# The side input's gate by seven block products in place of eight, in an fp32 two-layer encoder on one core

## The reference, cut to what matters

```python
for i in range(DEPTH):                       # DEPTH = 2, D_MODEL = 1024
    h = h + mixer(rmsnorm(h, norm_mix_g[i]))
    h = h + expert_choice_moe(rmsnorm(h, norm_ffn_g[i]), ...)
    gate = sigmoid(rmsnorm(h, norm_ple_g[i]) @ ple_w_gate[i])     # (256 x 1024) @ (1024 x 1024), twice
    h = h + (p[i] @ ple_w_proj[i]) * gate
return rmsnorm(h, final_norm_g)
```

## Time and profile before

| | |
|---|---|
| Median of 3 runs | 1766.92 us (1766.44 to 1767.38) |
| The profiled execution's own time | 1766.45 us |
| Its span, first to last instruction and transfer | 1764.7 us |
| PE busy | 1636.6 us (93%) |
| DVE, ACT, POOL busy | 572.2, 453.6, 133.0 us |
| Mean granted TensorE clock | 0.982 of 2.4 GHz |
| Read from HBM | 446.87 MB |

### The profile page before, as it was taken

One profiled execution on the slowest core, in us unless ns is written; L12 is line 12 of the kernel. 1 busy time (PEld: TensorE's weight loads), 2 busy tenths in 40 slices (PEclk: granted clock), 3 DMA queues, 4 the chain that ended last, 5 costly groups with the idle time before them and its releaser, 6 DMA issues.

```text
span 1764.7 us, 21301 instructions
## 1 busy us (share of the span) xinstructions
PE 1636.6 (93%) x9045; PEld 847.3 (48%) x9045; DVE 572.2 (32%) x1030; ACT 453.6 (26%) x990; POOL 133.0 (8%) x113
## 2 busy tenths in 40 slices
PE   7999899999889979999999899898999998899788
PEld 4464544443233324578875677854444432333233
DVE  3562311121201213388971356633111212012032
ACT  3232211101011105422125565442111010111053
POOL 2000000000000002052404231000000000000000
PEclk9999999999999999999999999999999999999999
DMA  7008379999999995012120000264799999999931
GB/s 251 1 1 333 120 316 427 427 427 428 427 425 427 428 424 191 1 48 96 50 94 1 1 3 2 97 282 171 286 428 427 427 429 428 424 427 428 426 132 48
DMA packets 50909, 450.34 MB, mean 255 GB/s; under 512 B 4931, under 2 KB 7199, under 8 KB 25599
## 3 DMA queue, kind: packets, MB, share of 16 engines
q1 hardware_dynamic: 50288, 448.67, 61.3%
q0 software_dynamic: 288, 0.22, 0.0%
q10 hardware_dynamic: 239, 0.09, 0.0%
HBM read 446.87 MB, written 2.10 MB: 254 GB/s over the span
## 4 chain that ended last, share of the span: by engine, by line
PE 68%; DMA 15%; DVE 7%; ACT 5%; issue 4%; POOL 1%; SPq 1%; DVEq 0%; ACTq 0%; POOLq 0%
PE banks L1830 28%; PE banks L1241 13%; DMA ring<-in_moe_w_up 7%; PE banks L1369 5%; DMA ring<-in_moe_w_down 5%; PE banks L1463 3%; PE banks L1721 3%; PE banks L1809 3%; PE banks L1858 2%; DVE misc L2171 2%; DMA ring<-in_moe_w_gate 2%; PE banks L1886 2%; PE banks L1324 1%; PE banks L1428 1%; PE banks L1513 1%
## 5 line engine op out<-in xcount | busy, mean ns | idle before, releaser
L1830 PE MATMUL banks<-ring,misc 128*64 128x512 f32 x2048 | 458.2, 598 | 34.0 <-DMA ring<-in_moe_w_up 21.0
L1830 PEld LDWEIGHTS banks<-ring,misc 128*64 128x64 f32 x2048 | 146.6, 138 | 318.3 <-issue 276.6
L1830 PE MATMUL banks<-ring,hid_t 128*64 128x512 f32 x976 | 217.5, 595 | 16.1 <-DMA ring<-in_moe_w_down 13.4
L1241 PE MATMUL banks<-ring,xt 128*128 128x512 f32 (+1 forms) x448 | 189.8, 585 | 1.0 <-ACT xt L830 0.5
L2537 DVE TENSOR_TENSOR work<-work,banks 128x512 f32<-128x512 f32 x32 | 33.6, 1052 | 476.7 <-PE banks L1830 476.7
L1191 ACT ACTIVATE misc<-banks 32x512 f32<-32x512 f32 x64 | 37.6, 587 | 458.3 <-PE banks L1830 457.9
L1830 PEld LDWEIGHTS banks<-ring,hid_t 128*64 128x64 f32 x976 | 68.4, 137 | 155.5 <-issue 138.1
L1241 PEld LDWEIGHTS banks<-ring,xt 128*128 128x128 f32 x448 | 84.8, 190 | 104.0 <-issue 102.9
L2552 DVE COPY misc<-banks 32x512 f32<-32x512 f32 x64 | 44.2, 691 | 226.0 <-PE banks L1830 225.6
L678 POOL TENSOR_TENSOR ring<-ring 128x1024 f32<-128x1024 f32 x24 | 59.6, 2486 | 738.9 <-DMA ring<-in_gdn_w_in 666.4
L2171 DVE SCALAR_TENSOR_TENSOR misc<-ring,conv_w,misc 128x512 f32<-128x512 f32 x96 | 92.2, 960 | 3.4
(11 more groups left out here) (327 smaller groups left out, 1677.0 us busy)
## 6 DMA issues: line engine op xcount, KB each, us to landing
ring<-in_moe_w_gate SPq DMA_DIRECT2D x64, 2048.0 KB, 22.3
ring<-in_moe_w_up SPq DMA_DIRECT2D x64, 2048.0 KB, 24.0
ring<-in_moe_w_down SPq DMA_DIRECT2D x58, 2048.0 KB, 25.0
ring<-in_gdn_w_in SPq DMA_DIRECT2D x8, 2048.0 KB, 8.4
ring<-in_ple_w_gate SPq DMA_DIRECT2D x4, 2048.0 KB, 21.4
ring<-in_moe_w_down SPq DMA_DIRECT2D x6, 1024.0 KB, 23.2
ring<-in_mla_w_out SPq DMA_DIRECT2D x2, 2048.0 KB, 23.4
misc<-in_moe_w_down SPq DMA_DIRECT2D x2, 2048.0 KB, 21.4
```

The costliest lines, as they stand in the source:

```text
L1241: mm = pe.matmul(psum[:, banks.bank(st, i), 0:cols], lhs(k), rhs(k), start=(k == 0), stop=(k == n - 1))
L1830: mm = pe.matmul(psum[64 * f:64 * f + 64, bank, :], tokens(4 * kh + k), w[k][:, k, f * HALF:(f + 1) * HALF], start=(kh == 0 and k == 0), s ...
```

## The change

```diff
+            def ple_pool(l):                              # POOL; l=0 ahead of gdn_pool(), l=1 behind it
+                b11, b12, b21, b22 = pg_w_in(l)
+                t1, t2 = pg_t(l)
+                pool.wait_ge(moe_sem["w_used"], NPIECE * (l + 1))
+                for f in range(2):
+                    wait_use(pool, f"ple_g{f}{l}")
+                pool.tensor_tensor(t1, b12, b11, ALU.subtract).then_inc(sum_weights, 1)
+                pool.wait_ge(sum_weights, 4 * l + 1)
+                pool.tensor_tensor(t2, b22, t1, ALU.subtract).then_inc(sum_weights, 1)
+                pool.tensor_tensor(b12, b22, b12, ALU.subtract).then_inc(sum_weights, 1)
+                pool.wait_ge(sum_weights, 4 * l + 3)
+                pool.wait_ge(*lay[l].s_pg.full(out_no(P2, 1) + 1))
+                pool.tensor_tensor(b21, b21, t2, ALU.subtract).then_inc(sum_weights, 1)
...
+        def norm_pair(act, name, sigmoid):                # ACT, blocks 2 and 3
...
+            for j in js:
+                sigmoid(j, 1)
+            for x, j in enumerate(js):
+                square(j, 1)
...                                                        # Identity with eps on the half's sum
+            sigmoid(NT, 0)
+            square(NT, 0)
+            sigmoid(NT + 1, 0)
+            act.activation(half_ss[:, 2 * NJ:2 * NJ + 1], eps[:, :], ACT.Sqrt)
+            root(NT, n + 5)
+            square(NT + 1, 0)
+            root(NT + 1, n + 7)
+            scaled(NT)
+            scaled(NT + 1)
...
-                for i in range(8):                        # ACT
-                    act.wait_ge(*L.s_pg.full(i + 1))
...
-                    act.activation(gate[:, i % 2, :], psum[:, banks.bank(L.s_pg, i), :],
-                                   ACT.Sigmoid).then_inc(L.s_pg.freed(i)[0], 1)
-                    if i % 2:
-                        load_sqrt()
-                        norm_act(act, ("mix1", "last")[l], i // 2)
+                for t in range(NT):
+                    copy_out(L.s_pg, out_no(P1, t), pg_p1[:, t, :])
...
+                for j, f in PLE_ORDER[0:4]:
+                    sigmoid(j, f)
+                load_sqrt()
+                for j in range(NT):
+                    norm_act(act, ("mix1", "last")[l], j)
+                norm_pair(act, ("mix1", "last")[l], sigmoid)
...
-                for key in (f"ple_g0{l}", f"ple_g1{l}"):  # PE
-                    wait_use(pe, key)
-                for i in range(8):
...
+                wait_use(pe, f"ple_g0{l}")
+                gate_product(P1, a11, b11)
+                L.s_pxt.wait_read(pe, KD - 1)
+                gate_product(P2, a12, b21)
+                pe.wait_ge(sum_tokens, 4 * l + 2)
+                pe.wait_ge(sum_weights, 4 * l + 2)
+                gate_product(P6, s2, t2)
+                gate_product(P5, s1, t1)
+                pe.wait_ge(sum_tokens, 4 * l + 4)
+                gate_product(P3, a12, b22)
+                pe.wait_ge(sum_weights, 4 * l + 4)
+                gate_product(P7, a21, b12)
+                gate_product(P4, a22, b21)
...
+                dve.tensor_tensor(s1, a21, a22, ALU.add)  # DVE; waits and counts left out here
+                dve.tensor_tensor(s2, s1, a11, ALU.subtract)
+                dve.tensor_tensor(a21, a11, a21, ALU.subtract)
+                for t in range(NT):
+                    gate_add(pg_c11[:, t, :], pg_p1[:, t, :], P2, t)
+                dve.tensor_tensor(a12, a12, s2, ALU.subtract)
+                for t in range(NT):
+                    gate_add(pg_q[:, t, :], pg_p1[:, t, :], P6, t)
+                for t in range(NT):
+                    gated_add(t, 0)
+                for t in range(NT):
+                    gate_add(pg_w[:, t, :], pg_q[:, t, :], P5, t)
+                for t in range(NT):
+                    gate_add(pg_c12[:, t, :], pg_w[:, t, :], P3, t)
+                    gated_add(t, 1)
...
+                for t in range(NT):
+                    norm(normed, t)
+                    gate_add(pg_w[:, t, :], pg_w[:, t, :], P7, t, False)
+                    gate_add(pg_q[:, t, :], pg_q[:, t, :], P7, t)
+                for t in range(NT):
+                    gated_add(NT + t, 1)
+                for t in range(NT):
+                    gate_add(pg_q[:, t, :], pg_q[:, t, :], P4, t)
+                    gated_add(NT + t, 0)
+                for t in range(NT):
+                    norm(normed, NT + t)
```

More of the change, by code:

```diff
@@ L120, in add, with skip @@
         self.order.append((stage, i))
+    def skip(self, n):
+        for _ in range(n):
+            self.order.append(self.order[-self.banks])
     def bank(self, stage, i):
@@ L414, in trunk_kernel @@
             if l == 1:
-                s_xt1 = stage("xt", KD, AV, before=prev.s_pxt)
+                s_xt1 = stage("xt", KD, AV, before=prev.s_pg)
                 s_ba = stage("gdn_ba", 1, ["dve"])
@@ L451, in trunk_kernel @@
             L.s_xt = stage("ffn_xt", KD, AV, before=s_xt1 if l else s_xt0)
-            L.s_lg = stage("router", 1, ["dve"], before=prev and prev.s_ib)
+            L.s_lg = stage("router", 1, ["dve"], before=prev.s_ib if l else s_vec)
             L.s_lgt = stage("router_t", 1, ["dve"], before=L.s_lg)
@@ L459, in trunk_kernel @@
             L.s_pxt = stage("ple_xt", KD, AV, before=L.s_xt)
-            L.s_pg = stage("ple_gate", 8, ["act"], before=prev and prev.s_pg)
+            L.s_pg = stage("ple_gate", 14, ["act"] * 2 + ["dve"] * 12, before=L.s_pxt)
+            banks.skip(2)
         vec_in, tab_in, out_done = sem("vec_in"), sem("tab_in"), sem("out_done")
@@ L773, in added, with square, root, scaled @@
             else:
-                eng.wait_ge(ple_added, 2 * NJ * int(prev[3]) + 2 * j + f + 1)
+                eng.wait_ge(ple_added, 2 * NJ * int(prev[3]) + PLE_ORDER.index((j, f)) + 1)
+        def norm_pair(act, name, sigmoid):
+            i = norm_no[name]
+            js = range(NT, NJ)
+            part = [half_ss[:, 2 * j:2 * j + 2] for j in js]
+            n = 4 * (NJ * i + NT)
+            def square(j, f):
+                added(act, name, j, f)
+                act.activation(work[:, f * HALF:(f + 1) * HALF], h[:, j, f * HALF:(f + 1) * HALF], ACT.Square, scale=1.0 / 32,
+                               accum_out=half_ss[:, 2 * j + f:2 * j + f + 1]).then_inc(sq_done, 1)
+            def root(j, count):
+                act.wait_ge(sq_done, count)
+                act.activation(rstd[:, j:j + 1], half_ss[:, 2 * j:2 * j + 1], ACT.Sqrt,
+                               bias=half_ss[:, 2 * j + 1:2 * j + 2]).then_inc(sq_done, 1)
+            def scaled(j):
+                if name != "last":
+                    act.wait_ge(rstd_done, NJ * i + j + 1)
+                    dst, src = half(j, 0, name)
+                    act.activation(dst, src, ACT.Copy, scale=rstd[:, j:j + 1]).then_inc(xn_act, 1)
+            for j in js:
+                sigmoid(j, 1)
+            for x, j in enumerate(js):
+                square(j, 1)
+                act.wait_ge(sq_done, n + 2 * x + 1)
+                act.activation(half_ss[:, 2 * j + 1:2 * j + 2], half_ss[:, 2 * j + 1:2 * j + 2], ACT.Identity,
+                               bias=eps[:, :]).then_inc(sq_done, 1)
+            sigmoid(NT, 0)
[7 more added lines that the diff above has]
+            scaled(NT + 1)
         def norm_act(act, name, j):
             i = norm_no[name]
-            for f in range(2):
+            f_last = 0 if name in ("mix1", "last") and j >= NT else 1
+            for f in (1 - f_last, f_last):
                 added(act, name, j, f)
@@ L2559, in _ @@
                 xt_out(dve, "dve", L.s_pxt, ROW_PLE + 8 * l)
[L2560 to L2573 removed]
+                a11, a12, a21, a22 = pg_tokens
```

94 lines of the change are left out of this document (69 added, 25 removed).

## The result

| | before | after |
|---|---|---|
| Median (runs, range), us | 1766.38 (8, 1764.73 to 1767.38) | 1773.41 (8, 1771.18 to 1777.40) |
| The profiled execution, us | 1766.45 | 1771.56 |
| Its span, us | 1764.7 | 1769.8 |
| Mean granted TensorE clock | 0.982 | 0.978 |

The ratio after to before is 1.0046, interval 1.0036 to 1.0056: slower by 7.0 us, more than the 0.2% that a measurement of this kernel can tell from nothing.

A forecast was written before the change was run, and what follows sets the result against it. The prediction took PE to bound the gate stage, with no slack behind it; its terms, -13.8 + 13.8 + 3.4 + 6.5 = +9.9 us, gave 1776.8 us, own range 1772 to 1782, 8 in 10 within 1768 to 1785.

The forecast's parts named there:

- Matmuls: Gate product: 56 matmuls in place of 64 in each layer, 6.9 us less a layer, -13.8 us in all.
- The start: Ahead of each gate: three POOL sums hold DVE's norm scalings, so the stage starts +7.1 us (layer 0), +6.7 (layer 1) later.
- The end of layer 1: After layer 1's last gate matmul: DVE has three times the work, last norm ends 9.0 us behind it, +3.4 us.
- DVE busy without a pause: Sign expected in the profile after: DVE has no pause over the last 12 us.
- The end of layer 0: After layer 0's gate: 22 more transposes stand behind block 2's norm, partly at a slow clock; +6.5 us, between +4 and +8.
- The mixer's sums and POOL's fourth: Beside the gate's matmuls: these POOL sums delay DVE's additions, but DVE catches up by P3's second output; nothing, up to 2 us otherwise.
- The sum: All terms: -13.8 + 13.8 + 3.4 + 6.5 = +9.9 us, giving 1776.8 us.
- scalings not held: Rival: POOL's sums hold DVE's norm scalings little or not, so the gate starts on time; -3.9, 1763.0 us; chance 0.12.
- reciprocal held: Rival: POOL's sums also hold the norms' 128x1 reciprocal ahead of the gate; +8 more, 1785 us; chance 0.1.
- ends that overlap better: Rival: start as forecast, but stage ends cost less (layer 1 +0.5, layer 0 +3); 1770.6 us; chance 0.12.
- wait for t2 or s2: Rival: POOL's weight sums come so late or long that PE waits for them in the gate; chance below 0.03.
- the end at E + 10: Layer 1's end: with a 1380 ns drain per ACT table load, the stage ends 10 us after the last gate matmul.

The follow-up runs named there:

- e1: The kernel before with the gate product over seven of its eight feature chunks, 56 matmuls a layer, nothing else: 1754.42 us, ratio 0.9941.
- e3: The changed kernel with one wait more: POOL starts its weight sums only after the last transposes ahead of the gate; 1764.21 us, ratio 0.9994.
- e8: The changed kernel with late POOL sums, block-by-block transposes, DVE additions between norms, mixer sums held until the last norm, six spare matmuls: 1766.10 us, ratio 1.0008.
- e2: Second experiment: the kernel before with only POOL's three 128x2048 weight sums added ahead of each gate, used by nobody; 1777.58 us, ratio 1.0067.
- e10: The kernel before with 223 spare waits in PE's program among layer 0's experts, nothing else; 1766.76 us, ratio 1.0001.
- e5: The kernel of e1 with eight spare fp32 matmuls at the start of PE's program; 1751.47 us, ratio 0.9914.

## Why the prediction was right, and where its sizes were off

The sign and the mechanism came as forecast: slower, since POOL's sums take at the start what the matmuls give, and the ends make the rest. The size was 7.0 us where +9.9 was forecast (1773.4 for 1776.8; the other 0.5 us is the kernel before, 1766.4 in eight runs for 1766.9 in three).

- **Matmuls**, -6.9 a layer: measured -6.94 in the kernel after, and -6.86 with nothing else changed (e1).
- **The start**, +7.1 and +6.7: measured +6.65 and +6.38. The term was too large by 0.8 in all. Three sums of 4.6, twice 0.3 us of turn-taking and 0.27 behind were to take 14.7 us; they took 14.12 (672.15 to 686.27). A sum is 4.50 where nothing holds it, and the turns cost 0.33 in all, not 0.6: from start to start there are 4.59 and 4.53 us. The 0.3 of rows 7 was that of L2171, an instruction of 0.75 us with two inputs; the scalings are 0.49 with one. t2 was ready 19 us before P6, not 10, as the forecast's own times give too (684.4 and 703.9). The Trainium skill, "SBUF — State Buffer", "SBUF: two separate sides", has DVE and POOL share ports under an exclusive lock, which a DVE instruction with two inputs takes only if both lie in SBUF. The trace agrees: the two additions with a PSUM input at 676.86 took 1.27 together inside POOL's sum L713.
- **The end of layer 1**, +3.4: measured +2.6. The order of events was the forecast's, step for step: norm(0)'s reciprocal at E - 8.7 for E - 8.8, the first addition of P4 ending at E - 0.2 for E + 0.5, norm(3)'s end at E + 8.2 for E + 9.0. The mis-sized term is the length of an instruction in a row of several. Two additions are 1.28 in a row of their own, but the next instruction starts 1.19 behind their start (1751.24, 1752.43). I added lengths where starts follow each other more closely; from norm(0)'s reciprocal to the end of P4's first addition it took 8.5 us instead of 9.3. "DVE busy without a pause" was not so: it has pauses of 1.03, 0.71 and 0.35 us behind E, all for ACT.
- **The end of layer 0**, +6.5: measured +6.2. Block 2's scaling was to end at E + 7.5, and 30 transposes start at E + 7.4. The granted clock in that window was 0.74 on average, between the levels of 1.2 and 2.4 GHz, and the transposes took 0.172 us each against 0.12 at the full clock. From the first of them to C it was 4.43 us, where before it was 0.51: 3.9 for the 22 that had come in between, 2.6 + 1.5 in the forecast.
- **The mixer's sums and POOL's fourth**, put at nothing: these were not free. The sums L734 begin at S + 18.5 and end at S + 30.1, as forecast, and hold DVE's first four gated instructions at 0.99 to 2.83. "By my count of its queue it has caught up" held in the kernel after: that addition starts at S + 34.6 in both layers, though only layer 0 has the mixer's sums; with the sums a little later against the stage (e3) it cost 2.8. The term was right by a margin that I had not worked out.
- **The sum.** Terms measured: -13.9 + 13.0 + 2.6 + 6.2 = +7.9. The medians say +7.0, and between the sum of the stages and the median the other kernels differ by up to 2.3 (e1), apart from e8, which slowed the mixer. So 2.0 of the 2.9 us are in the terms, and the last 0.9 is in what varies between executions.

The rivals: scalings not held (1763.0), out by the second experiment; reciprocal held, out by its 0.16 in every trace; ends that overlap better (1770.6), a tenth of its way in layer 0, over a quarter in layer 1. With 1773.4 the time lies about halfway between the forecast and this rival; that it came so near is in part what varies between executions. PE did not wait for t2 or s2.

ACT's table load in the end of layer 1 went from 1762.11 to 1763.40, and the next activation began with its end. No drain stands in the rows beside it, and the end at E + 10 did not come, which the prediction worked out from the figures of the Trainium skill, "ScalarE: Activation LUTs", "What ACT_TABLE_LOAD costs" (1283 ns and a drain of 1380).

**Open.** Why the stretch between the stages varies from 940.8 to 947.1 us (e8 left out) in kernels whose engines do the same work there, and why PE pauses 1.8 to 3.2 us in some of them. The kernels before, e2 and e10, with eight products, have none; all the others do, except e5.

## What to carry to other kernels

Work put on an idle engine is not free if it holds the instructions of an engine on the critical chain: here a POOL sum of 4.5 us turns each DVE scaling of 0.49 us that it meets into one of 2.7 to 4.6 us, and a norm's chain meets one per block. Before adding such sums, list which DVE instructions without an operand in PSUM fall into their time (the reciprocal of 128x1 was free), and give that work to ACT or start the sums behind them; then look where the sums that were behind have gone, since in e3 and e8 the hold that had moved cost something at a new place. And when matmuls are shortened, forecast the end of the stage by the queues of all the engines behind it, by the distance of starts.

## What the runs showed of the hardware

- A POOL sum of 128x2048 took 4.50 us alone, 5.4 to 5.5 when it alternates with DVE sums of 128x1024 (which took 3.6 to 5.4 instead of 1.2).
- The hold is not in proportion to the size of DVE's instruction: one of 128x64 is recorded with 5.15 us (e8), a scaling of 128x512 with 4.60 at most (e2). It goes by when POOL's instruction ends, and DVE ends behind that by more the more it has to do: 0.28 us for a scaling of 128x512 (0.49 alone), 0.55 for a two-input instruction of that size (0.69 alone), 1.08 for one of 128x1024 (1.22 alone; the last two in e3).
- A reciprocal of 128x1 took 0.16 us inside POOL's sums, as at 678.65 in the kernel after. ACT's copies with a scale took 0.71 beside them.
- Executions of one kernel scatter by some 3 to 4 us to either side, also in code that is the same, while the stages around the gate repeat to 0.2 us.
